# Second block's input norm from side sums, a two-tile opening of its product, low parts on GpSimd, and a third weight slot

## The reference

```
def first_block(x, ...):
    ...
    h = rms_norm(x, norm_ffn_pre[l])
    f = (jax.nn.silu(h @ w_ffn_gate[l]) * (h @ w_ffn_up[l])) @ w_ffn_down[l]
    x = x + rms_norm(f, norm_ffn_post[l])
    return x

def second_block(x, norm1_g, w_in, ...):
    h = rms_norm_2(x, norm1_g[l])
    z = h @ w_in[l]
    a, gate, q, k, v = jnp.split(z, splits, axis=-1)
    ...
```

## Time and profile before

| | us |
|---|---|
| median of 3 runs | 1456.29 |
| lowest and highest | 1455.47, 1456.39 |
| the profiled execution, its own time | 1456.94 |
| its span (first to last instruction) | 1455.2 |
| TensorE busy | 1444.2 (99%) |
| VectorE busy | 677.4 (47%) |
| GpSimd busy | 653.8 (45%) |
| ScalarE busy | 585.4 (40%) |

### The profile page before, as it was taken

How to read it: one execution, slowest core, us unless ns; L and a number is a source line. 1 busy time by engine, 2 the same in 40 slices (tenths; PEclk the granted TensorE clock), 3 DMA queues, 4 the chain that set the end, 5 groups by cost and what they waited for, 6 DMA issues and landing times.

```text
span 1455.2 us, 19531 instructions
## 1 busy us (share of the span) xinstructions
PE 1444.2 (99%) x7020; PEld 1171.3 (80%) x7020; DVE 677.4 (47%) x1093; ACT 585.4 (40%) x922; POOL 653.8 (45%) x304
## 2 busy tenths in 40 slices
PE   9999999999999999999999999999999999999999
PEld 6888888788788778888888887777678888888887
DVE  6426656775525285333331018989664333333000
ACT  5243435665643253332232225666654223222221
POOL 4434324762244434444444452766134444444443
PEclk9999999999999999999999999999999999999999
DMA  5422211111133223233233333322122223323333
GB/s 188 148 88 87 87 58 58 45 59 59 46 100 101 96 78 96 93 101 99 89 101 101 114 103 131 102 65 66 45 76 99 96 92 101 100 88 101 105 111 118
DMA packets 38573, 134.15 MB, mean 92 GB/s; under 512 B 4496, under 2 KB 4752, under 8 KB 38512
## 3 DMA queue, kind: packets, MB, share of 16 engines
q1 hardware_dynamic: 37248, 130.70, 27.5%
q10 hardware_dynamic: 1264, 2.62, 0.6%
HBM read 131.20 MB, written 2.10 MB: 92 GB/s over the span
## 4 chain that ended last, share of the span: by engine, by line
PE 74%; issue 14%; DVE 5%; POOL 4%; ACT 1%; DMA 0%; POOLq 0%; SPq 0%; DVEq 0%
PE bank L1177 18%; PE bank L1178 18%; PE bank L1179 18%; POOL wL L497 4%; PE bank L1530 3%; PE bank L1532 2%; PE bank L1531 2%; PE bank L1206 1%; PE bank L1208 1%; PE bank L1207 1%; PE bank L1309 1%; PE bank L1307 1%; PE bank L1308 1%; DVE bank L2291 1%; PE bank L1585 1%
## 5 line engine op out<-in xcount | busy, mean ns | idle before, releaser
L497 POOL TENSOR_TENSOR wL<-raw,wH 128x1024 fp32r<-128x1024 f32 x234 | 574.1, 2453 | 745.6 <-ACT wH L593 620.5
L593 ACT ACTIVATE wH<-raw 128x1024 fp32r<-128x1024 f32 x209 | 221.3, 1059 | 586.5 <-PE bank L1179 520.4
L1177 PE MATMUL bank<-aH,wH 128*128 128x512 f32 x920 | 359.5, 391 | 0.4 <-POOL wL L497 0.4
L1179 PE MATMUL bank<-aH,wL 128*128 128x512 f32 x920 | 358.0, 389 | 0.0
L1178 PE MATMUL bank<-aL,wH 128*128 128x512 f32 x920 | 358.0, 389 | 0.0
L1177 PEld LDWEIGHTS bank<-aH,wH 128*128 128x128 f32 x920 | 172.7, 188 | 38.7 <-issue 1.0
L1178 PEld LDWEIGHTS bank<-aL,wH 128*128 128x128 f32 x920 | 172.7, 188 | 36.2 <-issue 0.5
L1179 PEld LDWEIGHTS bank<-aH,wL 128*128 128x128 f32 x920 | 172.7, 188 | 35.8
L1179 PE MATMUL bank<-fH,wL 128*128 128x512 f32 x352 | 137.0, 389 | 0.0
L1178 PE MATMUL bank<-fL,wH 128*128 128x512 f32 x352 | 137.0, 389 | 0.0
L1177 PE MATMUL bank<-fH,wH 128*128 128x512 f32 x352 | 136.9, 389 | 0.0
(11 more groups left out here) (346 smaller groups left out, 1995.4 us busy)
## 6 DMA issues: line engine op xcount, KB each, us to landing
raw<-in_w SPq DMA_DIRECT2D x234, 512.0 KB, 3.3
bmk<-in_bias SPq DMA_DIRECT2D x6, 512.0 KB, 4.7
out_x<-xT SPq DMA_DIRECT2D x8, 256.0 KB, 3.6
xT<-in_x SPq DMA_DIRECT2D x3, 512.0 KB, 8.2
ct<-in_ct ACTq DMA_DIRECT2D x3, 384.0 KB, 3.7
xT<-in_x SPq DMA_DIRECT2D x2, 256.0 KB, 4.3
raw<-in_w SPq DMA_DIRECT2D x2, 256.0 KB, 4.7
w1k<-in_w1k ACTq DMA_DIRECT2D x1, 512.0 KB, 4.4
```

The costliest lines, as they stand in the source:

```text
L497: pool.tensor_tensor(wL[:, c_slot, :], raw[:, c_slot, :], wH[:, c_slot, :].bitcast(F32), ALU.subtract).then_inc(sem("w_lo"), 1)
L593: act.activation(wH[:, s, :], raw[:, s, :], ACT.Copy).then_inc(sem("w_hi"), 1)
L1177: pe.matmul(bank[:], hi, H[:, ka, :], start=(k == 0), stop=False)
L1179: mm = pe.matmul(bank[:], lo, H[:, ka, :], start=False, stop=(k == p.k - 1))
```

## The change

- **Sums ahead.** While `dn1` runs, VectorE also keeps sum over tiles of g^2 f^2 (`squares_of_z`, in `nt_`) and of g f x (`products_with_x`, in `nr`), for the tiles 0 to 6; the last tile's products go from `sq` straight through TensorE. `side_sums`, one-column matmuls, bring them and the old mean square (`nx`) to 128x4 tiles in `B[6]`. `idle_products` around this spread and the eight `add_up` products and squares are gone.
- **Root.** After kt = 3 VectorE does five steps on 128x4 tiles, ScalarE Ln and Exp after kt = 4, VectorE three steps after kt = 7, TensorE spreads the root into `B[4]`, ScalarE copies it to `nr`.
- **Residual.** Its product goes through two banks instead of `tmp`.
- **Low parts.** ScalarE writes the full value of each tile to `tmp` (in place of the square), GpSimd subtracts `aH` from it: `aL`.
- **Opening.** Tiles 0 and 1 advance together: for each kt four high products, and two low products two kt behind.
- **Third slot.** `mH`, unused until later, holds high and low part of the chunk of tile 2; both are made before the residual starts. The slots 0 and 1 then serve tiles 4, 6, ... and 3, 5, ... as before.

```diff
+        third_hi, third_lo = (mH[:, 2 * i:2 * i + 2, :].rearrange("p a s -> p (a s)") for i in range(2))
+        squares_of_z, products_with_x = nt_, nr
+        side_squares, side_products, side_mean, side_log, side_guess = (B[6][:, TT * i:TT * (i + 1)] for i in range(5))
+        def residual_bank(kt):
+            return B[(PH["in2"].t0 + 2 + kt % 2) % NBANK]
...
@@ SyncE
-                            sp.wait_ge(sem("ffn1_done"), 1)
+                            sp.wait_ge(sem("res2"), KD)
...
@@ GpSimd
-            pool.wait_ge(sem("ffn1_done"), 1)
+            pool.wait_ge(sem("w_hi"), i2 + 3)
+            pool.tensor_tensor(third_lo, raw[:, i2 % 2, :], third_hi.bitcast(F32), ALU.subtract).then_inc(sem("w_lo"), 1)
+            for kt in range(KD):
+                pool.wait_ge(sem("h3_hi"), kt + 1)
+                pool.wait_ge(sem("h3_x"), kt + 1)
+                pool.tensor_tensor(aL[:, kt, :], tmp[:, kt % 2, :], aH[:, kt, :].bitcast(F32), ALU.subtract)\
+                    .then_inc(sem("h3_lo"), 1)
+            pool.wait_ge(sem("res2"), KD)
...
@@ ScalarE
-            high_of_x("h3", "g_norm1", "res2", 4, True)
-
             p = PH["in2"]
+            act.wait_ge(sem(f"w_landed{p.c0 % 2}"), 16 * (p.c0 // 2 + 2))
+            act.wait_ge(sem("chunk_done"), p.c0)
+            act.activation(third_hi, raw[:, p.c0 % 2, :], ACT.Copy).then_inc(sem("w_hi"), 1)
+            for kt in range(KD):
+                act.wait_ge(sem("res2"), kt + 1)
+                act.activation(aH[:, kt, :], xT[:, kt, :], ACT.Copy, scale=vec("g_norm1", kt)).then_inc(sem("h3_hi"), 1)
+                if kt >= 2:
+                    act.wait_ge(sem("h3_lo"), kt - 1)
+                act.activation(tmp[:, kt % 2, :], xT[:, kt, :], ACT.Copy, scale=vec("g_norm1", kt)).then_inc(sem("h3_x"), 1)
+                if kt == 4:
+                    act.wait_ge(sem("side_ready"), 4)
+                    act.activation(side_log, root_x, ACT.Ln).then_inc(sem("ln_ready"), 1)
+                    act.wait_ge(sem("ln_ready"), 5)
+                    act.activation(side_guess, side_log, ACT.Exp, scale=-0.5).then_inc(sem("nr_ready"), 1)
+            act.wait_ge(sem("root_spread"), 3)
+            act.activation(nr[:], B[4][:], ACT.Copy).then_inc(sem("nr_ready"), 1)
...
-            rsqrt(5, B[6][:], D, (sem("sum_ready"), 5), nr[:], B[5][:])
             act.preload_act_table_set("sigmoid_and_others")
...
@@ TensorE
-            idle_products(1)
+            def side_sums(out, src, col, start=False):
+                for t in range(TT):
+                    mm = pe.matmul(out[:, t:t + 1], src[:, t * P:(t + 1) * P], col, start=start and t == 0, stop=True,
+                                   skip_group_check=True)
+                return mm
+            pe.wait_ge(sem("side_ready"), 1)
+            side_sums(side_squares, sq[:, 1, :], squared_gains[:, KD - 1:KD], True)
             spread_root(2, B[5])
-            idle_products(2)
+            pe.wait_ge(sem("side_ready"), 3)
+            side_sums(side_squares, squares_of_z, ones[:, 0:1])
+            side_sums(side_mean, nx, ident[:, 0:1])
...
+            for k in range(KD):
                 high_products(k)
+                if k == 0:
+                    side_sums(side_products, products_with_x, ones[:, 0:1])
+                if k == 1:
+                    side_sums(side_products, sq[:, 0, :], vec("g_ffn_post", KD - 1)).then_inc(sem("sum_ready"), 1)
                 if k >= 2:
+                    pe.wait_ge(sem("h3_lo"), k - 1)
+                    for t in range(2):
+                        low_product(t, k - 2)
+            spread_root(3, B[4])
+            for t in range(2):
+                for k in range(KD - 2, KD):
+                    pe.wait_ge(sem("h3_lo"), k + 1)
+                    mm = low_product(t, k)
+                mm.then_inc(sem("chunk_done"), 1)
...
@@ VectorE
+                if t == KD - 1:
+                    dve.tensor_tensor(sq[:, 0, :], bank[:], xT[:, t, :], ALU.mult).then_inc(sem("side_ready"), 1)
+                dve.tensor_copy(z2T[:, t, :], bank[:]).then_inc(sem("bank_free"), 1)
...
             token_root(4, B[4], D, narrow(B[5]))
-            residual_and_low(z2T, "g_ffn_post", "res2", "h3", "g_norm1", 2, True)
-            dve.wait_ge(sem("res2"), KD)
-            dve.sem_inc(sem("ffn1_done"), 1)
-            norm(5, B[6], B[5])
+            for kt in range(KD):
+                dve.scalar_tensor_tensor(residual_bank(kt)[:], z2T[:, kt, :], vec("g_ffn_post", kt), B[5][:], ALU.mult, ALU.mult)\
+                    .then_inc(sem("res2_mul"), 1)
+                dve.wait_ge(sem("res2_mul"), kt + 1)
+                dve.tensor_tensor(xT[:, kt, :], residual_bank(kt)[:], xT[:, kt, :], ALU.add).then_inc(sem("res2"), 1)
+                if kt == 3:
+                    dve.wait_ge(sem("sum_ready"), 5)
+                    link(dve.tensor_tensor(root_x, side_squares, root, ALU.mult))
+                    link(dve.scalar_tensor_tensor(root_x, side_products, 2.0, root_x, ALU.mult, ALU.add))
+                    link(dve.tensor_tensor(root_x, root_x, root, ALU.mult))
+                    link(dve.scalar_tensor_tensor(root_x, root_x, 1.0 / D, side_mean, ALU.mult, ALU.add))
+                    dve.tensor_scalar(root_x, root_x, EPS, None, ALU.max).then_inc(sem("side_ready"), 1)
+            dve.wait_ge(sem("nr_ready"), 5)
+            link(dve.tensor_tensor(root_t, side_guess, root_x, ALU.mult))
+            link(dve.scalar_tensor_tensor(root_t, root_t, -0.5, side_guess, ALU.mult, ALU.mult))
+            dve.scalar_tensor_tensor(root, root_t, 1.5, side_guess, ALU.add, ALU.mult).then_inc(sem("root_ready"), 1)
+            dve.wait_ge(sem("nr_ready"), 6)
```

110 lines of the change are left out of this document (62 added, 48 removed).

## The result

The changed kernel is slower: 1459.07 us against 1455.81 (medians of 20 executions each), a ratio of 1.0022 with a 95% interval of 1.0016 to 1.0029. The forecast was 1452.7. The profiled execution took 1458.27, its span is 1456.2 against 1455.2.

What follows compares the result with a forecast made beforehand. TensorE, busy 99% of the span, was taken as the bound. Starting tile 2 at 891.5 instead of 895.14 gives 3.6 us, with nothing counted behind it: 1456.3 - 3.6 = 1452.7 us, range 1450.9 to 1455.0.

Steps and rivals of the forecast that it cites:

- The two side sums behind the spread: Between root spread and first high product: replace two idle products; start 876.05 at full clock, 876.9 at half, against 876.12.
- The third slot: Conversion (1.06 us) and subtraction (2.40) for tile 2's chunk, about 872.4 to 876.5: hidden where ScalarE and GpSimd were nearly idle.
- The residual through PSUM: VectorE's residual in the opening: keeps its pace of 1.38 us per kt, at no cost.
- The longer steps in `dn1`: VectorE in `dn1`: four more steps per tile, under 8 us, beside a 15 us tile: cost nothing.
- I take the low level from 873.4 to about 880: TensorE's clock at the seam: half speed over that time loses 1.55 us, putting tile 2 at 891.7.
- the slower rival: Clock stays low through the opening: slower if it returns after 886.8, up to +8.4 us, 1464.7; chance 0.07.
- The sums don't do it: Rival: late side sums hold VectorE at kt = 3, adding up to 1.5 us to its chain, giving 892.7; inside the range.
- The blocked narrow step: Behind kt = 3, VectorE's step reading two SBUF tiles waits for GpSimd: 0 to 1.3 us, taken as 1.0; `max` 0.3.
- I count nothing for it: In `in2`, the second `up`, held by GpSimd's chunk: VectorE is back at TensorE's 3.6 us shift there, no loss charged.
- TensorE waits inside `in2`: Sign that the forecast is wrong: TensorE idle inside `in2`, behind the seam.
- the two chains: Opening up to tile 2: TensorE's chain ends at 891.7, that of VectorE, ScalarE and GpSimd at 891.2; 891.5 taken.
- full blocking: Upper case of VectorE's narrow steps waiting for GpSimd: tile 2 at 892.3 on the VectorE, ScalarE and GpSimd chain.

Runs made afterwards that it cites:

- e14: Changed kernel without the four side sums behind the spread and behind k-blocks 0 and 1 (output not the reference's): 1456.88 us, 1.0000 of the kernel before.
- e7: Changed kernel with root copy from the bank, early sigmoid table, and both inner side sums moved ahead of k-block 0: 1455.78 us, 0.9994 of the kernel before.
- e11: e9 with the copy to `nrc` reading `nr` in SBUF again: 1453.33 us, 0.9982 of the kernel before.
- e12: e9 with the sigmoid's table loaded late again, behind `nr`: 1454.04 us, 0.9980 of the kernel before.
- e9: Changed kernel with two idle products behind the spread, side sums behind k-blocks 1 to 4, narrow steps after kt = 7, bank copy, early table: 1453.74 us, 0.9981 of before.
- e13: e9 with both the SBUF copy and the late table again: 1457.29 us, 1.0005 of the kernel before.
- e6: e7 plus one idle product ahead of the spread and one behind it: 1455.60 us, 0.9993 of the kernel before.
- e10: e9 without its two idle products behind the spread: 1457.99 us, 1.0012 of the kernel before.
- e2: Changed kernel with the copy to `nrc` reading the spread root's bank instead of `nr` in SBUF: 1457.45 us, 1.0008 of the kernel before.
- e1: Changed kernel with three dense idle products back: ahead of the spread, behind it, and between two side sums: 1458.55 us, 1.0016 of the kernel before.
- e4: Kernel before the change, without its three idle products at this seam: 1457.24 us, 1.0002 of the kernel before.
- e8: e3 without the early load of the sigmoid's table: 1455.72 us, 0.9998 of the kernel before.
- e3: Changed kernel with three dense idle products, copy to `nrc` from the bank, and early sigmoid table: 1455.12 us, 1.0002 of the kernel before.

## Why the prediction was wrong

**What held.** The two side sums behind the spread were no loss: the first high product came at 875.38, 6.26 behind the token sums. The sum had 876.9 (7.15) for it, at the low level; by its full-clock figure, 876.05, it would be 6.30. The clock fell only inside the second of the two sums, and both took 2.58 us. The third slot was hidden (GpSimd's 2.37 us at 873.32, ahead of its first low part at 875.99). The residual through PSUM kept 1.39 per kt. GpSimd made low parts 1.36 apart (5.43 / 4), forecast 1.35. The longer steps in `dn1` cost nothing: it ended no later. TensorE's work fits as well: 18.9 us from the first product to tile 2, less half of the 11.8 us at the low level in it, are 13.0 for a forecast of 13.3.

**The step that failed: "I take the low level from 873.4 to about 880".** It began at 873.7 and lasted to 887.1, which is 874.3 to 887.8 on the scale of the trace of before (0.63 more). The reasoning was that "the rise has to wait until some k-blocks have run", and against the slower rival that "from the third k-block on no one-column sums are left". What I missed is what the low level does to its own length: at half clock the side sums behind k-blocks 0 and 1 last 1.56 each and the third k-block starts at 882.2, not 879. So the thin stretch reached 882.2, and the clock rose 4.9 us behind it. e14 shows that the sums do it: without them the low time is 6.8 us. That it is the two between the k-blocks isn't shown: in e7, where these stand ahead of the first product, the thin stretch ended at 879.3, the rise still came 5.9 us later, and the low time was the same 13.7.

**The rival had the right sum.** "It passes 895.14 if the clock comes back later than 886.8": on the scale of before it came back at 887.8, and tile 2 stands at 894.88 (894.25 + 0.63). By its formula (876.9 + 13.3 + half of 876.9 to 887.8) it would be 895.6. The pricing was right within 0.8 us, most of it the start that came 0.9 earlier; the chance of 0.07 was too low. The trace showed a fall and a return only with dense idle products around them, and I took their return time for a kernel without any.

**"The sums don't do it" came true along with it.** VectorE stood 3.73 at kt = 3, priced at up to 1.5. The sums' end at the low level had been put at 882, near where it was (882.2, or 882.8 on the scale of before), but of the 2.7 us from VectorE's 879.3 to there only 1.5 were charged. It cost nothing by itself: the last low part was done at 891.67 (887.71 + 3.96), and TensorE reached the last of its products at 894.0.

**The blocked narrow step was right as a mechanism, and wrong in place.** Forecast: the third of the five narrow steps, over 0.5 us. After, all took 0.16 to 0.17, since GpSimd had run dry for want of `xT`. Where it hadn't, the third step took 1.24 in e11 and 1.22 in e12, and the fifth, `max` with one SBUF input, 1.17 in e9 and 1.34 in e13. In e6 both were held (1.14, 1.16); in e10 neither was, as GpSimd's last low part ended when the third step began (886.1). VectorE's narrow steps, then GpSimd's low parts beside them, of e9:

```profile
885.45 0.17 DVE L2333 TENSOR_TENSOR roots<-roots 128x4 f32<-128x4 f32 x1
...
885.85 1.17 DVE L2335 TENSOR_SCALAR roots<-roots 128x4 f32<-128x4 f32 x1
```

```profile
882.93 4.06 POOL L568 TENSOR_TENSOR aL<-tmp,aH 128x512 fp32r<-128x512 f32 x3
```

It ends at 887.02, GpSimd at 886.99. I had taken 0.3 for that step, between 0 and 1.35: it was 0.17 where the third step had been held (e11, e12), and most of the upper end where that one had gone free (e9, e13). That a step goes free by starting in GpSimd's short gap between two instructions fits these rows; it wasn't tested.

**"I count nothing for it" failed too.** I had followed the two `up` steps up to GpSimd's chunk and not the copy to `nrc` behind them. The copy was 0.34 us ahead of the chunk before (901.63, 901.97): a gap of that size between two instructions that exclude each other is a bound, not a margin. Counted from the token sums the copy now came 0.67 later (32.55 for 31.88), because VectorE's first tile did (25.04 for 23.36), and GpSimd's chunk 0.24 earlier. The order turned round, and the held copy moved a chain to tile 6 that had no room. "TensorE waits inside `in2`" was named as a sign of failure, at another place. This second step cost 1.75 us in the profile.

**Two slips in the sum.** With the two chains at 891.7 and 891.2 the later one bounds tile 2, so the sum was 891.7 (3.4 earlier) and not 891.5; and full blocking, 0.3 and 1.05 on top of 891.2, is 892.5, not 892.3. Neither matters beside the 3.3 us between the 3.6 forecast and the 0.26 measured.

**What stays open.** The medians differ by 3.3 us, the profiles by 1.3. The clock accounts for more in executions that weren't profiled: at 0.994 the low level lasts (1 - 0.994) x 2 x 1456 = 17.5 us, of which the seam has 13.7 and a stretch near 505 us, in code that the change doesn't touch, 3.4 (the row below). At 0.991 or 0.992, six of the twenty executions, at 1460.3 to 1463.4 us, it is 23 to 26. Candidates are in the other profiles. e2, with the opening of the changed kernel, was low for 17.1 us at the seam. e13 fell behind its wait at tile 6. And 9 of the 17 profiles (e1, e2, e4, e6, e8, e9, e10, e13, e14) have 3.4 us at the low level near 995 us, in code that no edit touches; from the head sums to the end they take 535.4 to 535.7 us, the other eight, before and after among them, 533.9 to 534.1. None of the three was seen in the changed kernel itself. The same question is open for e3, e8 and e10, whose slowest executions (1459.5 to 1461.8) weren't profiled. Stretch of the kernel after, then the stretch near 995 us of e9 (with the low level) and of e11 (without), columns as above:

```profile
500.00:510.00 10.00, 9.75 (x40) 6.45 (x39) 5.59 (x12) 3.43 (x6) 2.90 (x2) 0.83 0.32 105
```

```profile
990.00:1000.00 10.00, 9.75 (x52) 7.59 (x51) 7.72 (x19) 6.82 (x16) 4.49 (x4) 0.83 0.18 54
```

```profile
990.00:1000.00 10.00, 9.75 (x61) 7.81 (x60) 8.75 (x20) 7.03 (x16) 4.50 (x4) 1.00 0.18 54
```

## What to carry to other kernels

Here one-column work on TensorE did least harm behind the point where dense products ran without a gap (e9), and most in front of or between the first of them. Price such work at half clock first, and ask what the longer low stretch does to its own length. Where a change moves one of two engines that share a port, list every instruction pair that was less than a microsecond from meeting, also far behind the edit. Useless products ahead of the first real ones can pay: two were worth 4.2 us in the medians between e10 and e9; three in the kernel before were worth nothing clear of the interval (e4). And look at the clock of every execution before a difference of 2 us between two profiles is put down to an edit.

## What the runs showed of the hardware

- Thin work at full busy share doesn't bring the clock back: TensorE was busy 100% of the stretch from 874.0 to 887.0 at a granted clock of 0.50. The first dense run without side sums in it began at 882.2, the rise came 4.9 us later (5.9 in e7). The Trainium skill (TensorE: Matmul & The Clock Gate, Part 1) speaks of how busy TensorE has been; the busy share of the profile is not a measure of that here.
- At the low level a product takes 0.43 us instead of 0.23, and a side sum of four fp32 one-column matmuls 1.56 instead of 0.82.
- A wait of TensorE of 1.84 us in otherwise dense work was followed by 3.4 us at the low level in two of four profiles that have it, and not in the other two.
- A VectorE copy of 128x512 fp32 from SBUF to SBUF, and narrow 128x4 steps with one or two SBUF inputs, waited for GpSimd's running instruction to its end (2.31 for 0.62; 1.17 in e9 and 1.24 in e11 for 0.17). The same copy out of PSUM took 0.68 in the middle of a GpSimd instruction (e2).
- Executions of one and the same kernel differ by a stretch of 3.4 us at the low level in code far from any edit: near 995 us it is in 9 of 17 profiles and makes the part behind the seam 1.6 us longer.
